# Hybrid encoder layer on one core: the barrier after attention and the order of work at the seam to the first feed-forward unit

## The reference

```
h = rms_norm(x, g_mix_pre); z = h @ w_in            -> pool group u | q | k | v
pool = (window mean - token) @ pool_w * pool_scale  (windows 2, 4, 8, 16)
q, k = axial_rope(rms_norm(q or k)); attn = softmax(q k^T / 8) v   (8 heads of 64, 2 key-value heads)
x = x + rms_norm(concat(pool, attn) @ w_out, g_mix_post)
h = rms_norm(x, g_ffn_pre)
x = x + rms_norm((silu(h @ w_gate) * (h @ w_up)) @ w_down, g_ffn_post)      (inner width 2816)
y = x + (p @ w_proj) * sigmoid(x @ w_pgate + b_pgate)
```

## Time and profile before

| | |
|---|---|
| median of 3 runs | 2388.13 us (2387.17 to 2389.5) |
| the profiled execution, its own time | 2387.49 us |
| its span, first to last instruction | 2385.7 us |
| mean granted TensorE clock | 0.988 |
| PE busy | 2306.7 us (97%), 10928 matmuls |
| DVE / ACT / POOL busy | 1675.4 / 1035.8 / 952.8 us |
| PE idle before the feed-forward products (L1383) | 28.8 us |
| PE idle before the mix stage's products | 16.2 us, in one piece |

### The profile page before, as it was taken

How to read it: one execution, slowest core, us unless ns; L and a number is a source line. 1 busy time by engine, 2 the same in 40 slices (tenths; PEclk the granted TensorE clock), 3 DMA queues, 4 the chain that set the end, 5 groups by cost and what they waited for, 6 DMA issues and landing times.

```text
span 2385.7 us, 29640 instructions
## 1 busy us (share of the span) xinstructions
PE 2306.7 (97%) x10928; PEld 1910.3 (80%) x10928; DVE 1675.4 (70%) x1753; ACT 1035.8 (43%) x1538; POOL 952.8 (40%) x557
## 2 busy tenths in 40 slices
PE   8999999999799979999999999899999999999999
PEld 6888788888678868888887888788788888877877
DVE  5766788888645668766766555887888865575842
ACT  4433688888643443333333222444343332233321
POOL 0000345554414654444543456454456634550200
PEclk9999999999999989999999999999999999999999
DMA  5223223222257873544447768555557687676431
GB/s 186 83 71 98 87 60 74 66 52 53 46 156 233 250 245 125 167 150 159 150 137 275 272 253 303 159 195 173 172 172 265 211 326 256 247 246 239 155 111 75
DMA packets 337374, 402.75 MB, mean 169 GB/s; under 512 B 36688, under 2 KB 240336, under 8 KB 337104
## 3 DMA queue, kind: packets, MB, share of 16 engines
q1 hardware_dynamic: 337232, 400.87, 51.1%
HBM read 259.18 MB, written 137.43 MB: 166 GB/s over the span
## 4 chain that ended last, share of the span: by engine, by line
PE 84%; DVE 7%; issue 2%; DMA 2%; ACT 2%; POOL 1%; SPq 1%; DVEq 0%; ACTq 0%; POOLq 0%
PE ps L1383 47%; PE ps L1175 32%; PE ps L1178 6%; DVE ring L2118 1%; DVE reg L2126 1%; DMA xb<-x_turned 1%; DVE negmax L2023 1%; DVE pt L2059 0%; DMA row_scales<-recip 0%; ACT pt L1485 0%; DVE fhi L2237 0%; DVE fb L2427 0%; POOL fb L1169 0%; DVE atb L2037 0%; DVE ev L2237 0%
## 5 line engine op out<-in xcount | busy, mean ns | idle before, releaser
L1383 PE MATMUL ps<-reg,ring 128*128 128x512 f32 x5544 | 1272.0, 392 | 28.8 <-DVE ring L2118 27.9
L1383 PEld LDWEIGHTS ps<-reg,ring 128*128 128x128 f32 x5544 | 1047.0, 189 | 252.6 <-DVE ring L2118 23.9
L1485 ACT ACTIVATE ring<-wraw 128x1024 fp32r<-128x1024 f32 (+2 forms) x152 | 143.7, 946 | 395.2 <-PE ps L1383 395.2
L2118 DVE TENSOR_TENSOR ring<-wraw,ring 128x1024 fp32r<-128x1024 f32 (+2 forms) x152 | 228.2, 1502 | 59.3 <-ACT ring L1485 58.6
L1175 PE MATMUL ps<-win,ht 128*128 128x512 f32 (+1 forms) x1152 | 227.7, 358 | 11.2 <-DVE win L1959 11.1
L1175 PEld LDWEIGHTS ps<-win,ht 128*128 128x128 f32 x1152 | 190.8, 191 | 41.9 <-issue 11.6
L1485 ACT ACTIVATE ring<-ws 128x1024 fp32r<-128x1024 f32 (+2 forms) x114 | 108.0, 947 | 238.7 <-PE ps L1383 235.9
L2059 DVE TENSOR_TENSOR pt<-ps,pt 128x512 fp32r<-128x512 f32 x256 | 174.3, 686 | 40.1 <-ACT pt L1485 36.9
L2118 DVE TENSOR_TENSOR ring<-ws,ring 128x1024 fp32r<-128x1024 f32 (+2 forms) x114 | 171.7, 1506 | 43.2 <-ACT ring L1485 42.5
L1175 PE MATMUL ps<-wout,ct 128*128 128x512 f32 x768 | 183.1, 397 | 16.2 <-DVE ct L2074 16.2
L1175 PEld LDWEIGHTS ps<-wout,ct 128*128 128x128 f32 x768 | 144.1, 191 | 46.6 <-DVE ct L2074 16.7
(11 more groups left out here) (204 smaller groups left out, 2916.7 us busy)
## 6 DMA issues: line engine op xcount, KB each, us to landing
reg<-ff_forms SPq DMA_DIRECT2D x42, 1536.0 KB, 9.6
ff_forms<-fhi SPq DMA_DIRECT2D x88, 512.0 KB, 3.2
wraw<-in_w_gate SPq DMA_DIRECT2D x88, 256.0 KB, 4.2
wraw<-in_w_up SPq DMA_DIRECT2D x88, 256.0 KB, 4.6
ff_forms<-ev SPq DMA_DIRECT2D x44, 512.0 KB, 2.9
wraw<-in_w_down SPq DMA_DIRECT2D x48, 384.0 KB, 5.3
reg<-ff_forms SPq DMA_DIRECT2D x14, 1024.0 KB, 6.9
xt_a<-in_xt SPq DMA_DIRECT2D x16, 512.0 KB, 4.5
```

Of the source, the lines that this page charges most:

```text
L1383: last = nc.tensor.matmul(ps[:, 2 * chain + m, :], ring[:, st % 3, a, m, k * P:(k + 1) * P], reg[:, k, i, e, :], start=OPENS[i] and k == 0 ...
L1485: copy = lambda out, src, **k: nc.scalar.activation(out, src, ACT.Copy, **k)
L2118: V.tensor_tensor(ring_block(u, st, 1), weight_source(u, i), f(ring_block(u, st, 0)), ALU.subtract).then_inc(S["w_split"], 1)
```

## The change

At the end of attention: TensorE counts on the barrier but does not wait for it (`stage_left`). ScalarE and VectorE make the halves of tile 0 and of strip 2 ahead of the barrier. SyncE loads strips 6 and 7, writes the last row scales and sends the last `ot` across ahead of it; the last sum of parts on GpSimd, the last two scalings on VectorE and the last two stores on SyncE come after it, between the preparations of the mix stage. `recip` moves to another place in memory. GpSimd waits for the last stores of attention before its per-tile loop.

At the seam: three weight blocks (not two) are split at tile 12, the fourth and fills 1 to 3 are moved ahead of the unit's loop and between the steps of tiles 14 and 15, the last three stay in the loop, two products later than before. SyncE stores the rows of a pair (3 forms) as soon as they are there, and each of GpSimd's four forms when it is made; the loads of the pieces stand between these stores.

The diff, cut to its core (empty lines left out; `concat_lo` on VectorE and `fill_lo`'s new argument `part`, which takes one of its pieces, are left out, as is the bound of `fill_hi` and `fill_lo` in the loop, from `m = st + 4` to `m = st + 2` with `m >= 4` for the first sequence):

```diff
@@ -224,6 +224,10 @@
             e.wait_ge(stage_done, 5 * stages[e])
             alone(e)
+        def stage_left(e):
+            stages[e] = stages.get(e, 0) + 1
+            e.drain().then_inc(stage_done, 1)
...
@@ -620,26 +624,31 @@
                         sp.wait_ge(*at_least(f"pl_out{half}", 16 * NH // 2))
                     sp.wait_ge(S["strip_split"], KT + 2)
                     mixed_in(0)
-            block_out(2 * NSEQ * NH - 1)
-            attended_out(2 * NSEQ * NH - 1)
-            stage_end(sp)
-
-            def residual_rows(n):
-
-                sp.dma_start(xs_d[:, n % 2, :], x[n // NT * NT + TILES[n % NT]]).then_inc(S[f"xd_in{n % 2}"], 16)
-
             for k in range(6, KT):
                 out_strip(k)
+            last = 2 * NSEQ * NH - 1
+            scales_through(last)
+            cross(last)
+            stage_end(sp)
+            def residual_rows(n):
+                sp.dma_start(xs_d[:, n % 2, :], x[n // NT * NT + TILES[n % NT]]).then_inc(S[f"xd_in{n % 2}"], 16)
             mixed_in(1)
+            attended_out(last - 1)
             sp.dma_start(gpost[:], g_mix_post.partition_broadcast(P)).then_inc(S["gains_in"], 16)
+            for half in range(2):
+                sp.wait_ge(*at_least(f"pl_out{half}", 16 * NSEQ * NH // 2))
             with nc.allow_non_contiguous_dma(reason="gain columns, loaded once"):
                 sp.dma_start(gffn[:], g_ffn_pre.rearrange("(k p) -> p k", p=P)).then_inc(S["gains_in"], 16)
             residual_rows(0)
             residual_rows(1)
             mixed_in(2)
+            scales_in(last)
+            attended_out(last)
             for half in range(2):
                 sp.wait_ge(*at_least(f"at_out{half}", 16 * NSEQ * NH))
-                sp.wait_ge(*at_least(f"pl_out{half}", 16 * NSEQ * NH // 2))
             def store(n):
...
-            def store_forms(pair):
+            def store_rows(pair):
                 s, o, b = pair // (NT // 2), pair % (NT // 2) * P, pair % 2
-                sp.wait_ge(S["h2_forms"], pair + 1)
-                for m, rows in ((0, h2a[:, b, 0:KG]), (5, h2a[:, b, KG:KT]), (3, h2b[:, b, KG:KT]),
-                                (1, forms[:, b, 0]), (2, forms[:, b, 1]), (4, forms[:, b, 2]),
-                                (6, forms[:, b, 3])):
+                sp.wait_ge(S["h2_out"], 2 * pair + 2)
+                for m, rows in ((0, h2a[:, b, 0:KG]), (5, h2a[:, b, KG:KT]), (3, h2b[:, b, KG:KT])):
                     sp.dma_start(h2f_d[s, :, m, :, o:o + P], rows).then_inc(S[f"h2_st{b}"], 16)
+            def store_forms(pair, which):
+                s, o, b = pair // (NT // 2), pair % (NT // 2) * P, pair % 2
+                for w in which:
+                    sp.wait_ge(S["h2_forms"], 4 * pair + w + 1)
+                    m, form = ((4, 2), (1, 0), (2, 1), (6, 3))[w]
+                    sp.dma_start(h2f_d[s, :, m, :, o:o + P], forms[:, b, form]).then_inc(S[f"h2_st{b}"], 16)
             def weights_in(u, m):
...
                     piece_in(0, 4)
                 if n == LAST:
-                    for q in range(6, 10):
-                        piece_in(0, q)
+                    break
                 store(n)
                 if n in (4, 6, 8):
                     sp.wait_ge(S["strip_split"], 2 * KT)
                     weights_in(UNITS[n // 8], n // 2 % 2 if n < 8 else 0)
                 if n >= 3 and n % 2:
-                    store_forms(n // 2 - 1)
-            for q in range(10, NP * len(fill_pieces(0))):
-                piece_in(0, q)
-            store_forms(NT - 1)
+                    store_rows(n // 2 - 1)
+                    store_forms(n // 2 - 1, range(4))
+                if n == LAST - 1:
+                    store_rows(NT - 2)
+                    for q in range(6, 9):
+                        piece_in(0, q)
+                    store_forms(NT - 2, range(3))
+            store(LAST)
+            store_forms(NT - 2, (3,))
+            piece_in(0, 9)
+            piece_in(0, 10)
+            piece_in(0, 11)
+            store_rows(NT - 1)
+            store_forms(NT - 1, (0, 1))
+            piece_in(0, 12)
+            store_forms(NT - 1, (2, 3))
+            piece_in(0, 13)
             sp.wait_ge(S["x1_stored"], NSEQ * NT * 16)
             for b in range(2):
                 sp.wait_ge(S[f"h2_st{b}"], 32 * NP * NSEQ)
...
@@ -1062,8 +1089,8 @@
                 if h:
                     add_parts(2 * h - 1)
             add_parts(2 * NSEQ * NH - 2)
+            stage_end(pool)
             add_parts(2 * NSEQ * NH - 1)
-            stage_end(pool)
             def sums(u, which):
...
                 alone(pool)
-                nc.gpsimd.tensor_tensor(made[:, 2], hi[:, KG:KT], hi[:, 0:KG], ALU.subtract)
-                go(nc.gpsimd.tensor_tensor(made[:, 0], hi[:, 0:KG], lo[:, 0:KG], ALU.subtract))
-                go(nc.gpsimd.tensor_tensor(made[:, 1], hi[:, KG:KT], made[:, 0], ALU.subtract))
-                nc.gpsimd.tensor_tensor(made[:, 3], lo[:, KG:KT], made[:, 1], ALU.subtract)\
-                    .then_inc(S["h2_forms"], 1)
+                nc.gpsimd.tensor_tensor(made[:, 2], hi[:, KG:KT], hi[:, 0:KG], ALU.subtract).then_inc(S["h2_forms"], 1)
+                nc.gpsimd.tensor_tensor(made[:, 0], hi[:, 0:KG], lo[:, 0:KG], ALU.subtract).then_inc(S["h2_forms"], 1)
+                pool.wait_ge(S["h2_forms"], 4 * pair + 2)
+                alone(pool)
+                nc.gpsimd.tensor_tensor(made[:, 1], hi[:, KG:KT], made[:, 0], ALU.subtract).then_inc(S["h2_forms"], 1)
+                pool.wait_ge(S["h2_forms"], 4 * pair + 3)
+                alone(pool)
+                nc.gpsimd.tensor_tensor(made[:, 3], lo[:, KG:KT], made[:, 1], ALU.subtract).then_inc(S["h2_forms"], 1)
             pool.wait_ge(S["gains_in"], 32)
             alone(pool)
+            for half in range(2):
+                pool.wait_ge(*at_least(f"at_out{half}", 16 * NSEQ * NH))
+                alone(pool)
+                pool.wait_ge(*at_least(f"pl_out{half}", 16 * NSEQ * NH // 2))
+                alone(pool)
             for n in range(NSEQ * NT):
                 pool.wait_ge(S["x1_out"], n + 1)
                 pool.wait_ge(S["h2_out"], n)
...
@@ -1309,7 +1344,7 @@
                     pooled(h)
             for j in range(4):
                 pv(2 * NSEQ * NH - 1, j)
-            stage_end(pe)
+            stage_left(pe)
             def mix_strip(n, c, k):
...
                 copy(w_out_at(k, 0), out_place(k)).then_inc(S["strip_hi"], 1)
+            def concat_hi(n):
+                act.wait_ge(*at_least(f"ct_in{n % 2}", 16 * (n // 2 + 1)))
+                if n >= 2:
+                    act.wait_ge(S["mix_done"], 2 * (n - 1))
+                copy(ct[n % 2][:, 0].rearrange("p k n -> p (k n)"), ctraw(n)).then_inc(S["c_hi"], 1)
             q_out(0, 0)
             q_out(0, 1)
             exp(0)
@@ -1654,14 +1695,11 @@
                 if u == 4 and NH + 2 <= h < NH + 4:
                     act.wait_ge(S["score_done"], NSTEP // 2)
                     out_strip(h - NH - 2)
+            concat_hi(0)
+            act.wait_ge(S["score_done"], NSTEP)
+            out_strip(2)
             o_out(2 * NSEQ * NH - 1)
             stage_end(act)
-
-            def concat_hi(n):
-                act.wait_ge(*at_least(f"ct_in{n % 2}", 16 * (n // 2 + 1)))
-                if n >= 2:
-                    act.wait_ge(S["mix_done"], 2 * (n - 1))
-                copy(ct[n % 2][:, 0].rearrange("p k n -> p (k n)"), ctraw(n)).then_inc(S["c_hi"], 1)
             def post_a(n):
                 act.wait_ge(S["mix_done"], 2 * (n + 1))
@@ -1683,9 +1721,9 @@
                 act.wait_ge(S["h2_ready"], n)
                 copy(x1t[:].rearrange("p k n -> p (k n)"), pair(5)).then_inc(S["x1_out"], 1)
-            concat_hi(0)
-            for k in range(2, KT):
+            for k in range(3, KT):
                 out_strip(k)
             def weights_hi(st):
                 u, i = UNITS[st // NP], st % NP
...
@@ -1799,18 +1837,21 @@
                         fill_hi(0, 0)
                     x1_out(n - 1)
                 if n == NSEQ * NT - 4:
-                    weights_hi(0)
-                    weights_hi(1)
+                    for st in range(3):
+                        weights_hi(st)
             fill_hi(0, 1)
             post_a(NSEQ * NT - 1)
+            fill_hi(0, 2)
             post_b(NSEQ * NT - 1)
             x1_out(NSEQ * NT - 1)
-            for st in range(-2, NST + 1):
+            weights_hi(3)
+            fill_hi(0, 3)
+            for st in range(NST + 1):
                 u, i = UNITS[min(max(st, 0) // NP, NU - 1)], st % NP
                 inside = 0 <= st < NST
                 if inside and i == 2:
                     middle(u)
-                if 0 <= st < NST - 2:
+                if 2 <= st < NST - 2:
                     weights_hi(st + 2)
                 if st and i == 0:
                     before = UNITS[st // NP - 1]
...
@@ -2065,15 +2112,10 @@
```

(27 more changed lines are left out.)

34 lines of the change are left out of this document (19 added, 15 removed).

## The result

The changed kernel takes 2377.23 us (median of 6 runs, 2374.5 to 2380.4) against 2389.89 (6 runs, 2387.17 to 2393.03) for the kernel before: ratio 0.9945, 95% interval 0.9936 to 0.9955. So 12.7 us are won, half of the 25.1 forecast; the time lies above the range. The profiled execution has a span of 2375.3 us at a mean clock of 0.991 (2385.7 and 0.988 before).

What follows compares the result with a forecast made beforehand. TensorE, busy 2306.7 of 2385.7 us, was taken as the bound, with only idle stretches and slow clock to win: 11.4 at the barrier plus 13.7 at the seam, 25.1 us, gave 2363 us, range 2356 to 2375.

Steps and rivals of the forecast that it cites:

- The barrier, 11.4 forecast: End of attention to mix stage: TensorE no longer waits at the barrier and tile 1 starts earlier; 11.4 us won.
- 0.69 and the low half, 1.2: Before tile 1: VectorE scales half head 31 (0.69 us), then makes tile 1's low half (1.2 us), giving 659.1.
- They are issued at 641.7 and have 5 us or more: Mix stage, tile 0: loads of w_out strips 6 and 7, issued at 641.7, have at least 5 us.
- SyncE is in time: Barrier: SyncE issues its other loads and stores by about 652.6, before the row scales' write lands at 654.2.
- Rival (a): Barrier: SyncE held up ahead of the scales' return, which lands 4 to 6 us later; 2368.5 us, chance 0.15.
- Used 3.0 us later: Barrier: the row scales are read back and used 3.0 us after SyncE goes on, at 657.2.
- VectorE now has the scaling of half head 31 in front of it: Barrier: tile 1's low half stands behind this 0.69 us scaling on VectorE; TensorE stalls 5.7 us before tile 1.
- The seam, 13.7 forecast: Seam to the first feed-forward unit: reordered weight blocks, fills and stores end unit 0 at 897.9, not 911.6; 13.7 us won.
- the two stalls in product 1: Seam: new TensorE idle of 1.0 us for a pushed-back piece and 2.6 us for VectorE's last per-token scale.
- VectorE has fill 4 ready at 878.3, TensorE asks at 878.4: Seam, product 4: fill 4 is ready in time by a margin of 0.1 us.
- rival (b): Seam: VectorE becomes the bound and products 4 and 5 wait 5 us; 2368 us, chance 0.12.
- about 5 us of the 13.7 back: Seam: the shared-port rule's cost if GpSimd were beside every piece of fills 2 to 6.

Runs made afterwards that it cites:

- e3: Changed kernel without the last write of row scales; half head 31 is scaled with half head 30's scales, so that output differs: 2370.44 us.
- e6: Changed kernel, SyncE waiting until strips 6 and 7 of w_out have landed before issuing the last write of row scales: 2383.11 us.
- e7: Changed kernel, GpSimd holding back the second feed-forward unit's weight sums until all seven forms of the first are filled: 2375.96 us.
- e8: Changed kernel, VectorE making tile 15's per-token scale ahead of fill 2 and not behind it: 2376.95 us.
- e10: Changed kernel with both seam moves: GpSimd's second-unit weight sums held back until seven fills are done, tile 15's scale ahead of fill 2: 2374.89 us.
- e9: Changed kernel, last row-scale write behind tile 2's landing, tile 3's load ahead of the read-back, half head 31 scaled after VectorE's tile 0 steps: 2364.04 us.
- e4: Changed kernel, VectorE making the low half of tile 1 ahead of the scaling of half head 31: 2368.33 us.
- e1: Only the barrier half of the change, on the kernel before: 2385.2 us, ratio 0.9983.
- e5: e3 with the scales read back right behind half head 30's store, ahead of gains, residual rows and tile 2: 2365.08 us.

## Why the prediction was wrong

The sum was 25.1 us and the stages give 2.8 + 8.5 = 11.3, so 13.8 are missing, and they are in the two terms. By the medians 12.7 are won and 12.4 missing; the stretches outside the two places differ by some 1 us between the two profiled executions.

**The barrier, 11.4 forecast, 2.8 measured.** Right: TensorE starts tile 0 at once; the release 2.1 us after attention (1.7 put); strips 3 to 6 in time but for 0.3 us in all (9.93 for 42 matmuls); "0.69 and the low half, 1.2", from the scales to tile 1, 2.0 us as put. Wrong steps:
- "They are issued at 641.7 and have 5 us or more", of strips 6 and 7. Strip 7 needed 14, 7 without the write (e3), about 6 with the write behind it (e6). The prediction cited that what is queued *behind* the write lands with it, and did not ask about what is just ahead. This put the gap of 6.63 us into tile 0, but it is not what cost the time: tile 1 was later still, and started as late in the runs where strip 7 took about 2 us less (e7, e8, e10).
- "SyncE is in time": by 652.6 at the return, 10.2 us after the end of attention. It came there at 656.25 (15.1), since the issue of the residual rows took 8.8 us, and issued the return at 15.2 instead of 11.8: 3.4 us. Rival (a), at 0.15, has SyncE held at this place; it was held not by the pooled store, as (a) has it, but by the issue of the rows. How much of the 3.4 is SyncE's and how much the write's own length (11.6 put) is not shown in after: the queue moves 77 GB/s in the window from 652 and 279 in that from 654, and the crossed rows, queued behind the write, are used at 655.58. By these rows, as an estimate, the write took 12.5 to 14 us, and SyncE came 0.7 to 2.2 us after it. In e9 SyncE goes on 10.9 us after the write.
- "Used 3.0 us later": 7.2, so 4.2 us. The price came from the earlier trace rows, where the queue was empty; in after it moved 336 GB/s (and in e9, with one load still under way, the read took 3.4). A duration of a transfer was carried over without the load around it.
- Together tile 1 started 7.6 us later than put. The slow clock behind its stall cost 2.7 us (13.94 against 11.20 for its 48 matmuls) and not 2.0: 0.58 granted in the window from 664, 0.56 in that from 668.

The head-of-line place itself was named ("VectorE now has the scaling of half head 31 in front of it") but its 0.69 us and all of the chain ahead of it were taken as unavoidable for tile 1. e4 shows that they were not: the place was worth 8.1 us.

By the rule cited from the Trainium skill ("DMA: Bandwidth & Descriptors", queues, rings and completion order) what is issued after the scales arrives no sooner than they. The traces agree: of what left after 641.54, the first use is at 655.58; and in before nothing moves from 646 to 652 (0 GB/s), while the store issued at 644.18 lands after 8.5 us. The rule, as cited, says nothing of the load ahead.

**The seam, 13.7 forecast, 8.5 measured.** Right: tile 12's block costs 1.1 (1.36 of idle against 0.23 in e1; 1.15 put); `turn_back` without a wait; products 2 and 3 without a wait; the two stalls in product 1, put at 1.0 and 2.6, measured 1.47 and 2.86; the clock, 1.8 put, 3.4 us at half speed in the windows from 860 and 864 (0.83 and 0.74), so 1.7. Wrong: "VectorE has fill 4 ready at 878.3, TensorE asks at 878.4". The margin of 0.1 us rested on 2.1 a piece beside GpSimd, taken from pieces beside form-making steps of 2.0 to 2.3 us. Here GpSimd does weight sums of 3.37 us, and a piece takes 3.40 and 3.19. This was rival (b), at 0.12, priced at 5: the waits at products 4 and 5 are 3.8 of the 5.2 by which the seam falls short; 0.7 more are the two stalls in product 1, and the rest is not assigned. e7 shows the cause: with GpSimd's sums away the pieces take 1.2 to 1.3 us.

The rule of the Trainium skill ("SBUF — State Buffer", shared port pair: VectorE and GpSimd take that port in turns, a whole instruction at a time) had been worked out in the prediction as "about 5 us of the 13.7 back" and was left out of the sum. The trace agrees: GpSimd's sums end at 875.51 and 878.84, the pieces beside them at 876.59 and 879.93, each 1.1 us after, close to the 1.2 of a piece alone.

**The rivals** (a) and (b) were given as alternatives to the forecast; (b) came, with 3.8 of its 5 us, and (a) in its effect, a return that is later than put. Independent mechanisms at two places don't exclude each other: with both, the sum of their prices was 2363 + 5.5 + 5 = 2373.5, inside the range. What carried the time past it is the barrier, which fell short by 8.6 and not 5.5: (a) has no term for a read-back that itself takes 7.2 us. The two had 0.27 between them, and what stood against them was a margin of 0.1 us and an argument on another wait.

Open: by what mechanism the write holds a load issued ahead of it, and how close is too close. The runs show only that strip 7, issued in the last half microsecond before the write, took 11.5 to 13.9 us in six runs, while in after strip 6, just ahead of it, had landed by 646.4 as without the write.

## What to carry to other kernels

When a wait is moved, list what stands behind it on its engine and put first what TensorE wants next; here one line was worth 8 us, more than the slow write or the late read-back. Give the price of a transfer together with the load of its queue at that time, and keep a scattered write of small elements away from loads that are due, on both sides of it. Where an engine is busy throughout a stretch, add up its work there with the neighbour's port time in it; a new order without less work moves the stall and doesn't remove it.

## What the runs showed of the hardware

- A write of 512 elements of 4 bytes (2 KB) is complete only 9.8 to 10.9 us after its issue, even when little or nothing else is in the queue (before, e9), and a 512 KB load issued 0.42 us behind it landed after 13.0 us (e9). It also held the second of two 512 KB loads issued just ahead of it: 11.5 to 13.9 us (e4, after) against 6 to 8 (e3, e6, e9).
- Meanwhile the DMA engines count as busy and move almost nothing: 16 GB/s at a share of 0.87 from 648 to 652 in after.
- Behind it the issuing itself stands still: SyncE took 6.8 to 9.4 us for two residual rows (e4, after, e6), against 2.5 to 3.8 without the write near (e3, before, e9, e5).
- The same 128 KB read-back was used 3.0 us after its issue in an empty queue (before), 3.4 with one load under way (e9), and 7.2 to 8.6 with 1.6 to 3.9 MB issued in the 10 us ahead of it (after, e5, e3, e4).
- A VectorE piece of 1024 columns with two inputs takes 1.2 us alone (e7), and beside GpSimd it ended 1.1 us after GpSimd's instruction, both for one of 3.37 us (after) and for one of 2.27 (before, 852.13 and 853.39).
